# Newton chains of three norms with their operand and intermediate in PSUM, and a first product by halves

## The chip, the cores and the metric

The kernel runs on one core of a Trainium2 chip. The metric is the device time of one execution in microseconds (us); lower is better. TensorE (PE) multiplies, VectorE (DVE), ScalarE (ACT) and GpSimd (POOL) do the elementwise work, and nearly all transfers are issued from SyncE's queue (SP).

## The reference

A hybrid encoder layer is applied to two sequences of 512 and 2048 tokens (2560 rows, D = 1024) in float32, with shared weights:

```
h    = rmsnorm(x, norm_g);  proj = h @ w_in                 # queries, keys, values, gates of all branches
o_a  = gla_branch(...)      # gated linear attention forward and backward, summed, rmsnorm over 128 per head
o_b  = diff_attention(...)  # softmax(s0) - lam * softmax(s1), times v, rmsnorm over 128 per head
o_c  = memory_cross_attention(...)                          # 256 memory tokens, normed with mem_norm_g
x    = x + (sum_i sigmoid(gate_i) * ((o_i * silu(z_i)) @ w_branch_i)) @ w_out
y    = rmsnorm(x, final_norm_g)
```

Each rmsnorm needs 1 / sqrt(mean square + eps) per row, or per row and head.

## The kernel before

The kernel is written engine by engine with explicit semaphores, as six phases one after the other; within a phase every engine works through its own list in order.

`phase_project` (0 to some 715 us of the profile) norms 20 tiles of 128 token rows and 4 of memory rows, transposes them on PE into `tp` (PSUM), splits each into a rounded high part (`h_hi`, ACT) and a rest (`h_lo`, DVE), splits the weights in the same way (`w_hi` or `wv_hi` by ACT or DVE, `w_lo` or `wv_lo` by POOL at L500), and forms each product from three matmuls (`product3`, L190 to L192). For one tile, `norm(n)` on DVE takes the sum of squares that ACT left in `stat` (L344), computes the reciprocal root (L440 and `rsqrt`, L180 to L185) and scales the tile into `xn` (L444). DVE's order at the start is norm 0, low 0, norm 1, norm 2, low 1, norm 3, low 2, low 3. PE's is transpose 0, the first product, transpose 1, product 1, transpose 2, and so on. Tile n+2 of x is loaded by SP only after norm n, in one queue with the weight pieces.

`phase_gla_forward` (to some 1825 us) and `phase_gla_backward` (to some 2107 us) run the recurrence tile by tile, and fill PE with dense products for the gates (`Dense`, L744), whose weights are split by ACT (L689) and POOL (L715). In the backward phase one tile is, on PE: `o_ps` (L1253), `d_ps` (L1257), 24 x 2 dense matmuls with a transpose (L1240) between. L1253 of a tile waits for DVE's state and sum (L1297, L1302) of the tile before. On DVE, in order: the gate product of the last dense unit (L704), state, `total` (L1302), its square (L1305), the reduction (L1306), the reciprocal root (L1307, then `rsqrt`), four scalings (L1312), L704 for the next unit, the gated output (L1278, L1280) and the gate (L1270). ACT's list holds a sigmoid of the gate tile `z` (L1331) ahead of the copies that DVE waits for (L1338). SP's list stores a dense unit after DVE's L704, then, at the end of a chunk of 8 units, issues 16 loads of h (L651, L652), then the next `z`, then the next tile.

`phase_diff` (some 2116 to 2843 us) makes scores on PE (L1579, L1580) into two PSUM buffers, which DVE empties with bias and maximum (L1718); ACT exponentiates; DVE and POOL combine the two softmaxes (L1741 on DVE, L1541 and L1545 on POOL); PE transposes and multiplies by v (L1593, L1604). Once in each group of 512 queries (20 groups, 16 of them of the long sequence) `normalise(g)` computes four reciprocal roots per row from `n_ps` (L1748, L1750, `rsqrt`), POOL builds a diagonal from them (L1557), PE spreads it (L1617), and DVE scales the output (L1761, L1764).

`phase_cross` and `phase_merge` follow. The merge has a fourth norm which the change leaves alone.

`rsqrt(step, dve, out, v, tmp)` is a first guess by integer arithmetic and three Newton steps: 11 DVE instructions on 1 or 4 elements per partition, each of which waits for the one before (`Chain`). All operands are columns of `stat` in SBUF.

Of the kernel before, what the change touches and what calls it, by code (L numbers as in the profile page):

```python
# [7 lines left out]
I32 = mybir.dt.int32  # L8
ALU = mybir.AluOpType
# [3 lines left out]
P = 128  # L13
D = 1024
KT = D // P
# [5 lines left out]
CH = 512  # L21
EPS = 1e-6
LAMBDA_INIT = 0.2

H = 4
GK = 64
GV = 128
# [150 lines left out]
def rsqrt(step, dve, out, v, tmp):  # L178

    step(dve.tensor_scalar(tmp.bitcast(I32), v.bitcast(I32), 1, None, ALU.logical_shift_right))  # L180
    step(dve.tensor_scalar(out.bitcast(I32), tmp.bitcast(I32), -1.0, float(0x5F3759DF), ALU.mult, ALU.add))
    for _ in range(3):
        step(dve.tensor_tensor(tmp, out, out, ALU.mult))
        step(dve.scalar_tensor_tensor(tmp, tmp, -0.5, v, ALU.mult, ALU.mult))
        step(dve.scalar_tensor_tensor(out, tmp, 1.5, out, ALU.add, ALU.mult))  # L185


# [8 lines left out]
def phase_project(nc, used, h, early, w_zg, w2, ident, x_all, gains, ident_dram, w_stream, w_narrow, w_values, w_mem, w_mem_values, hT_hi, hT_lo, featT, featT_lo, narrowT, values,  # L196
                  memkT, mem_v):

    with ExitStack() as ctx:
        m = Mem(nc, ctx, "proj")  # L200
        HD = 64
        BANKS, TT, COLS, SLOTS, OUTS, NC = 4, CH // P, W // P, 2, 3, TOK // CH
# [27 lines left out]
        h_hi, h_lo = h  # L230
# [3 lines left out]
        wv_hi, wv_lo = (m.sb(f"wv_{s}", [P, 2, KT, W], FP32R) for s in ("hi", "lo"))  # L234
        out = m.sb("out", [P, OUTS, CH])
# [5 lines left out]
        stat = m.sb("stat", [P, 2, 4])  # L241
        acc = m.ps("acc", [P, BANKS, CH])
        tp = m.ps("tp", [P, 2, 2, 512])
# [3 lines left out]
        hi_resident = m.sem("hi_resident")  # L247
# [8 lines left out]
        lo_ready = m.sem("lo_ready")  # L256
# [176 lines left out]
        def _(dve):  # L433
            def norm(n):
                b = n % 2
                step = Chain(dve, steps, n * (RSQRT_STEPS + 1))
                dve.wait_ge(squares, n + 1)
                if n in (0, TOK // P):
                    dve.wait_ge(mem_gain_in if n else gain_in, 16)
                step(dve.tensor_scalar(stat[:, b, 1:2], stat[:, b, 0:1], 1.0 / D, EPS, ALU.mult, ALU.add))  # L440
                rsqrt(step, dve, stat[:, b, 2:3], stat[:, b, 1:2], stat[:, b, 3:4])
                if n >= 2:
                    dve.wait_ge(transposed, n - 1)
                dve.scalar_tensor_tensor(xn[:, b], x[:, b], stat[:, b, 2:3], gain[:, 1 if n >= TOK // P else 0], ALU.mult, ALU.mult).then_inc(normed, 1)  # L444
# [58 lines left out]
        def _(pe):  # L503
# [8 lines left out]
            def first_product():  # L512
                tok = slice(0, P)
                pe.wait_ge(hi_ready, 1)
                pe.wait_ge(hi_resident, COLS)
                for k in range(KT):
                    pe.matmul(acc[:, 0], h_hi[:, 0, k, tok], wv_hi[:, 0, k], start=k == 0, stop=False)
                pe.wait_ge(lo_ready, 1)
                for k in range(KT):
                    pe.matmul(acc[:, 0], h_lo[:, 0, k, tok], wv_hi[:, 0, k], start=False, stop=False)  # L520
                pe.wait_ge(lo_split, COLS)
                for k in range(KT):
                    done = pe.matmul(acc[:, 0], h_hi[:, 0, k, tok], wv_lo[:, 0, k], start=False, stop=k == KT - 1)
                done.then_inc(unit_done, 1)
# [596 lines left out]
def phase_gla_backward(nc, used, h, early, ahead, ident, v_dram, o_dram, qb_dram, kb_dram, decb_dram, gain_dram, item_hi, item_lo, hT_hi, hT_lo, w_zg, zg):  # L1121

    with ExitStack() as ctx:
        m = Mem(nc, ctx, "glab")
        S, L, PAIRS = 2, 3, H // 2
# [7 lines left out]
        v = m.sb("v", [P, L, H, GV])  # L1133
# [5 lines left out]
        stat = m.sb("stat", [P, 4, H])  # L1139
# [7 lines left out]
        t_ps = m.ps("t_ps", [P, S, H, P])  # L1147
# [12 lines left out]
        gated = m.sem("gated")  # L1160
# [105 lines left out]
        def _(dve):  # L1266
# [15 lines left out]
            for n in range(N):  # L1282
                b = n % L
# [17 lines left out]
                step = Chain(dve, steps, n * STEPS + 1)  # L1301
# [2 lines left out]
                                       o[:, b].rearrange("p (a z v) -> p z a v", z=2, v=GV), ALU.add))  # L1304
                step(dve.tensor_tensor(sq[:, :, :], total[:, :, :], total[:, :, :], ALU.mult))  # L1305
                step(dve.tensor_reduce(stat[:, 0], sq[:, :, :], AXX, ALU.add))  # L1306
                step(dve.tensor_scalar(stat[:, 1], stat[:, 0], 1.0 / GV / GK, EPS, ALU.mult, ALU.add))  # L1307
                rsqrt(step, dve, stat[:, 2], stat[:, 1], stat[:, 3])
                if n >= S:
                    dve.wait_ge(turned, n - S + 1)  # L1310
                for h in range(H):
                    done = dve.scalar_tensor_tensor(normed_o[:, n % S, h], total[:, h], stat[:, 2, h:h + 1], gain[:, :], ALU.mult, ALU.mult)  # L1312
                done.then_inc(normed, 1)
# [39 lines left out]
def phase_diff(nc, used, ahead, front, ident, v_dram, lambda_dram, gain_dram, zg, item_hi, item_lo):  # L1353

    with ExitStack() as ctx:
        m = Mem(nc, ctx, "diff")
        HD, G, LAG, TMAX, KC, SLOTS = 64, 4, 5, max(SEQS), 512, 3
# [11 lines left out]
        k, q_high, q_low, table = ahead.k, ahead.q_high, ahead.q_low, ahead.table  # L1369
        p = front.p  # L1370
        v = m.sb("v", [P, 2, TMAX // P, P])
# [18 lines left out]
        stat = m.sb("stat", [P, 4, G])  # L1390

        s_ps = m.ps("s_ps", [P, 2, 2, KC])
        t_ps = m.ps("t_ps", [P, 2, G * P])
# [303 lines left out]
        def _(dve):  # L1697
# [46 lines left out]
            def normalise(g):  # L1744
                step = Chain(dve, norm_steps, g * NORM_STEPS)
                if g:
                    dve.wait_ge(diag_ready, g)
                step(dve.scalar_tensor_tensor(stat[:, 0], sums[:, g % 4, :, 0], EPS, sums[:, g % 4, :, 0], ALU.mult, ALU.mult))  # L1748
                dve.wait_ge(squares_summed, g + 1)
                step(dve.scalar_tensor_tensor(stat[:, 1], n_ps[:, 0:G], 1.0 / P, stat[:, 0], ALU.mult, ALU.add))  # L1750
                rsqrt(step, dve, stat[:, 2], stat[:, 1], stat[:, 3])

            def scale_output(g):
                dve.wait_ge(spread, g + 1)
# [680 lines left out]
```

## Time and profile before

| | |
|---|---|
| median of 3 runs | 3529.4 us (3525.36 to 3530.46) |
| profiled execution, its own time | 3529.79 us |
| its span, first to last instruction | 3528.0 us |
| PE busy | 3374.4 us (96%) |
| DVE busy | 2072.1 us (59%) |
| ACT busy | 1329.8 us (38%) |
| POOL busy | 1216.9 us (34%) |
| mean granted clock of TensorE | 0.982 |

The profiled execution is 1.8 us longer than its span (what lies around it) and 0.4 us above the median of the runs. A busy share is an average over six phases; which engine is late in a phase is read from the waits of that phase.

### The profile page before, as it was taken

To read this page: it belongs to the slowest core of one execution; us is meant where nothing else is said; L and a number is where in the kernel's file an instruction comes from. 1 tells how busy PE (TensorE), PEld (TensorE's weight loads), DVE (VectorE), ACT (ScalarE), POOL (GpSimd) and SP (SyncE) were. 2 spreads that over 40 slices of the span, in tenths; PEclk is the share of its full clock that TensorE was granted. 3 is DMA by queue.
4 is the path that set the end of the run, shared out by engine and by line. 5 is a ranking of instruction groups with operands and counts; after the bars stand their busy time and mean duration, and the time that the engine had idled before them with its cause. 6 is when DMAs were issued, how large, how long until landed. Compare 5 with 4: busy or idle time off the path is not lost. (4 is left out here: it accounts for less than half of the span.)

```text
span 3528.0 us, 46814 instructions
## 1 busy us (share of the span) xinstructions
PE 3374.4 (96%) x16944; PEld 2629.1 (75%) x16944; DVE 2072.1 (59%) x4688; ACT 1329.8 (38%) x2165; POOL 1216.9 (34%) x511
## 2 busy tenths in 40 slices
PE   7999999999999999999999987999999978999998
PEld 5888888877888888888877774666666555888887
DVE  3322312226646655665658788988988745666554
ACT  2111111123433433343323235666666645333332
POOL 2322412343333333333333335676677623000000
PEclk9999999999999999999999998999999999999999
DMA  6544545463453543543348975121221165676662
GB/s 205 178 155 178 178 151 177 165 232 122 140 176 119 180 138 118 176 134 125 121 142 275 303 226 154 57 81 37 72 61 54 42 242 203 238 239 199 200 215 81
DMA packets 317891, 554.64 MB, mean 157 GB/s; under 512 B 35421, under 2 KB 114525, under 8 KB 317662
## 3 DMA queue, kind: packets, MB, share of 16 engines
q1 hardware_dynamic: 266510, 471.26, 40.8%
q10 hardware_dynamic: 51152, 80.38, 6.3%
q8 instruction: 136, 2.23, 0.3%
q14 instruction: 93, 0.76, 0.1%
HBM read 382.03 MB, written 169.50 MB: 156 GB/s over the span
## 5 line engine op out<-in xcount | busy, mean ns | idle before, releaser
L715 POOL TENSOR_TENSOR glaf_w_lo<-early_raw,glaf_w_hi 128x1024 fp32r<-128x1024 f32 x140 | 345.9, 2471 | 711.8 <-ACT glaf_w_hi L689 711.8
L744 PE MATMUL glaf_dense_acc<-h_hi,glaf_w_hi 128*128 128x512 f32 x1120 | 452.6, 404 | 4.1 <-ACT glaf_dense_out L698 4.1
L744 PE MATMUL glaf_dense_acc<-h_lo,glaf_w_hi 128*128 128x512 f32 x1120 | 439.3, 392 | 0.0
L744 PE MATMUL glaf_dense_acc<-h_hi,glaf_w_lo 128*128 128x512 f32 x1120 | 437.5, 392 | 0.0
L1718 DVE CUSTOM_DVE_ANT_0 front_p<-diff_s_ps,ahead_table 128x512 f32<-128x512 f32 x544 | 345.6, 686 | 49.6 <-PE diff_s_ps L1580 47.6
L500 POOL TENSOR_TENSOR proj_w_lo<-early_raw,proj_w_hi 128x1024 fp32r<-128x1024 f32 x84 | 204.4, 2436 | 479.3 <-DVE proj_w_hi L462 479.3
L1541 POOL TENSOR_SCALAR front_p<-front_p,diff_ratio 128x1024 f32<-128x1024 f32 (+1 forms) x80 | 269.0, 3362 | 174.3 <-DVE diff_ratio L1738 174.3
L1661 ACT ACTIVATE front_p<-front_p,diff_neg_max 128x2048 f32<-128x2048 f32 (+1 forms) x160 | 278.8, 1743 | 38.5 <-DVE diff_neg_max L1728 38.4
L1579 PE MATMUL diff_s_ps<-ahead_k,ahead_q_high 128*128 128x512 f32 x544 | 246.7, 453 | 34.6 <-DVE diff_mx L1718 25.4
L1604 PE MATMUL diff_oT_ps<-diff_aT,diff_v 128*128 128x512 f32 x544 | 273.8, 604 | 6.2 <-ACT diff_aT L1655 6.2
L1110 DVE COPY_PREDICATED glaf_att<-glaf_picked,glaf_att_ps 128x256 f32<-128x256 int32 x280 | 147.3, 526 | 216.5 <-PE glaf_att_ps L876 209.7
L190 PE MATMUL proj_acc<-h_hi,proj_w_hi 128*128 128x512 f32 x672 | 262.8, 391 | 0.0
L192 PE MATMUL proj_acc<-h_hi,proj_w_lo 128*128 128x512 f32 x672 | 261.6, 389 | 0.0
L191 PE MATMUL proj_acc<-h_lo,proj_w_hi 128*128 128x512 f32 x672 | 261.5, 389 | 0.0
L744 PEld LDWEIGHTS glaf_dense_acc<-h_hi,glaf_w_hi 128*128 128x128 f32 x1120 | 211.9, 189 | 53.9 <-issue 7.9
L744 PEld LDWEIGHTS glaf_dense_acc<-h_hi,glaf_w_lo 128*128 128x128 f32 x1120 | 211.1, 188 | 46.2
L744 PEld LDWEIGHTS glaf_dense_acc<-h_lo,glaf_w_hi 128*128 128x128 f32 x1120 | 212.3, 190 | 40.3
L1593 PEld LDWEIGHTS diff_t_ps<-all_ident,diff_a 128*128 128x128 f32 x1088 | 134.2, 142 | 122.9 <-issue 99.3
L1580 PE MATMUL diff_s_ps<-ahead_k,ahead_q_low 128*128 128x512 f32 x544 | 218.6, 402 | 0.0
L1655 ACT ACTIVATE diff_aT<-diff_t_ps 128x512 f32<-128x512 f32 x272 | 158.9, 592 | 150.9 <-PE diff_t_ps L1593 150.9
L382 ACT ACTIVATE proj_out<-proj_acc 128x512 f32<-128x512 f32 (+1 forms) x93 | 55.7, 598 | 413.7 <-PE proj_acc L192 395.4
L462 DVE CAST proj_w_hi<-early_raw 128x1024 fp32r<-128x1024 f32 x84 | 59.6, 715 | 250.1 <-PE proj_acc L192 250.1
(215 smaller groups left out, 7385.5 us busy)
## 6 DMA issues: line engine op xcount, KB each, us to landing
early_raw<-in_w_zg SPq DMA_DIRECT2D x180, 512.0 KB, 4.4
early_raw<-in_w_stream SPq DMA_DIRECT2D x80, 512.0 KB, 3.6
scratch_zg<-glaf_dense_out SPq DMA_DIRECT2D x140, 256.0 KB, 2.3
items_raw<-in_w_br SPq DMA_DIRECT2D x120, 256.0 KB, 2.9
merge_gate<-scratch_zg SPq DMA_DIRECT2D x120, 256.0 KB, 3.2
scratch_featT<-proj_out ACTq DMA_DIRECT2D x80, 256.0 KB, 2.2
items_br_hi<-scratch_item_hi SPq DMA_DIRECT2D x60, 256.0 KB, 5.8
items_br_lo<-scratch_item_lo SPq DMA_DIRECT2D x60, 256.0 KB, 6.6
```

What stands on the lines that cost most here:

```text
L190: pe.matmul(out, a_hi, b_hi, start=first, stop=False)
L191: pe.matmul(out, a_hi, b_lo, start=False, stop=False)
L192: return pe.matmul(out, a_lo, b_hi, start=False, stop=last)
L500: pool.tensor_tensor(lo, raw_of(n), hi, ALU.subtract).then_inc(lo_split, 1)
L715: pool.tensor_tensor(self.w_lo[:, s], self.raw[:, u % self.RAW], self.w_hi[:, s], ALU.subtract).then_inc(self.lo_split, 1)
L744: done = pe.matmul(self.acc[:, u % self.banks], a, x, start=i == 0, stop=i == self.PER - 1)
L1541: pool.tensor_scalar(p[:, o.slot, 1, half], p[:, o.slot, 1, half], ratio[:, o.slot:o.slot + 1], None, ALU.mult).then_inc(far_scaled, 1)
L1579: pe.matmul(s_ps[:, chunk % 2, i], q_high[:, b, i, cols], k[:, key % KS, i], start=True, stop=False)
L1580: done = pe.matmul(s_ps[:, chunk % 2, i], q_low[:, b, i, cols], k[:, key % KS, i], start=False, stop=True)
L1604: pe.matmul(oT_ps[:, :], v[:, o.head % 2, kt], aT[:, unit % 2], start=kt == 0, stop=kt == o.nk - 1).then_inc(values_done, 1)
L1661: act.activation(p[:, o.slot, i, 0:o.T], p[:, o.slot, i, 0:o.T], ACT.Exp, bias=neg_max[:, o.slot, i:i + 1], scale=SLOPES[o.h], accum_out=s ...
L1718: dve.tensor_tensor_reduce(out=p[:, n.slot, i, c * KC:(c + 1) * KC], in0=s_ps[:, (n.c0 + c) % 2, i], in1=table[:, start:start + KC], scale ...
```

## The change

The two norms that are computed from SBUF (projection, backward) and the one that already reads PSUM (difference attention) now write the mean square `v` to PSUM and keep the intermediate `tmp` there; only the result stays in SBUF. The Newton step is reordered; each of its two-input instructions now has one input in PSUM or both. The PSUM columns are borrowed: `tp` of the tile's own buffer in the projection, `t_ps` of the tile's own buffer in the backward phase, columns 4 to 11 of `n_ps` in difference attention. Two waits come with that: `lo_ready` in the projection, and in the backward phase `gated`, with the old wait on `turned` moved ahead of the chain. The first product of the projection starts as soon as the first 256 of its 512 weight columns are there.

```diff
+def rsqrt_by_psum(step, dve, out, v, tmp):
+    step(dve.tensor_scalar(tmp.bitcast(I32), v.bitcast(I32), 1, None, ALU.logical_shift_right))
+    step(dve.tensor_scalar(out.bitcast(I32), tmp.bitcast(I32), -1.0, float(0x5F3759DF), ALU.mult, ALU.add))
+    for _ in range(3):
+        step(dve.scalar_tensor_tensor(tmp, v, -0.5, out, ALU.mult, ALU.mult))
+        step(dve.tensor_tensor(tmp, tmp, out, ALU.mult))
+        step(dve.scalar_tensor_tensor(out, tmp, 1.5, out, ALU.add, ALU.mult))
...
-                step(dve.tensor_scalar(stat[:, b, 1:2], stat[:, b, 0:1], 1.0 / D, EPS, ALU.mult, ALU.add))
-                rsqrt(step, dve, stat[:, b, 2:3], stat[:, b, 1:2], stat[:, b, 3:4])
+                if n >= 2:
+                    dve.wait_ge(lo_ready, n - 1)
+                v, tmp = (tp[:, b, 0, i:i + 1] for i in range(2))
+                step(dve.tensor_scalar(v, stat[:, b, 0:1], 1.0 / D, EPS, ALU.mult, ALU.add))
+                rsqrt_by_psum(step, dve, stat[:, b, 2:3], v, tmp)
...
-                pe.wait_ge(hi_resident, COLS)
-                for k in range(KT):
-                    pe.matmul(acc[:, 0], h_hi[:, 0, k, tok], wv_hi[:, 0, k], start=k == 0, stop=False)
+                for half in range(2):
+                    cols = slice(half * CH // 2, (half + 1) * CH // 2)
+                    pe.wait_ge(hi_resident, (half + 1) * COLS // 2)
+                    for k in range(KT):
+                        pe.matmul(acc[:, 0, cols], h_hi[:, 0, k, tok], wv_hi[:, 0, k, cols], start=half == 0 and k == 0, stop=False)
...
-                step(dve.tensor_scalar(stat[:, 1], stat[:, 0], 1.0 / GV / GK, EPS, ALU.mult, ALU.add))
-                rsqrt(step, dve, stat[:, 2], stat[:, 1], stat[:, 3])
                 if n >= S:
+                    dve.wait_ge(gated, n - S + 1)
                     dve.wait_ge(turned, n - S + 1)
+                var, tmp = (t_ps[:, n % S, 0, i * H:(i + 1) * H] for i in range(2))
+                step(dve.tensor_scalar(var, stat[:, 0], 1.0 / GV / GK, EPS, ALU.mult, ALU.add))
+                rsqrt_by_psum(step, dve, stat[:, 2], var, tmp)
...
-                step(dve.scalar_tensor_tensor(stat[:, 1], n_ps[:, 0:G], 1.0 / P, stat[:, 0], ALU.mult, ALU.add))
-                rsqrt(step, dve, stat[:, 2], stat[:, 1], stat[:, 3])
+                var, tmp = (n_ps[:, i * G:(i + 1) * G] for i in range(1, 3))
+                step(dve.scalar_tensor_tensor(var, n_ps[:, 0:G], 1.0 / P, stat[:, 0], ALU.mult, ALU.add))
+                rsqrt_by_psum(step, dve, stat[:, 2], var, tmp)
```

## Rows read from the trace of the kernel before

In rows 1 the columns are: stretch, its length, busy us (and instructions) of PE, PEld, DVE, ACT and POOL, granted clock, DMA share, GB/s. In rows 2: who waited for whom, us in total, times, longest. In rows 3: line, engine, operation, count, duration in ns as min/median/max, first and last start, form. In rows 4 to 6: start, duration in us, engine, line, form, count, and in brackets the idle time before and what ended it.

**Rows 1.** Busy time by stage: projection, backward phase, long groups of difference attention.
```profile
60.00:710.00 650.00, 650.00 (x2948) 534.16 (x2947) 164.71 (x405) 114.26 (x196) 188.54 (x78) 1.00 0.49 172
1825.00:2107.00 282.00, 265.47 (x1358) 211.59 (x1359) 226.54 (x518) 85.40 (x118) 99.52 (x41) 0.95 0.82 270
2222.00:2798.00 576.00, 561.84 (x2484) 374.78 (x2483) 517.70 (x1447) 388.26 (x514) 401.91 (x147) 1.00 0.18 54
```
**Rows 2.** PE's waits, in the stretches 0:60, 1815:2130 and 2130:2880.
```profile
PE proj_tp L509 <- DVE proj_xn L444: 12.6, 2, 9.9
...
PE glab_o_ps L1253 <- DVE glab_total L1302: 5.2, 2, 4.7
PE glab_dense_acc L744 <- POOL glab_w_lo L715: 4.1, 2, 2.5
...
PE diff_s_ps L1579 <- DVE diff_mx L1718: 22.5, 35, 2.9
```

**Rows 3.** DVE's durations by line, over the whole span.
```profile
L181 DVE TENSOR_SCALAR diff_stat<-diff_stat x20: 170/2320/2328, 2148.6 to 2835.3; 128x4 int32<-128x4 int32 x20
L1307 DVE TENSOR_SCALAR glab_stat<-glab_stat x20: 170/838/2299, 1840.6 to 2102.6; 128x4 f32<-128x4 f32 x20
L1750 DVE SCALAR_TENSOR_TENSOR diff_stat<-diff_n_ps,diff_stat x20: 160/161/163, 2148.2 to 2834.9; 128x4 f32<-128x4 f32 x20
L704 DVE TENSOR_TENSOR glab_dense_out<-glab_dense_acc,glab_dense_out x40: 676/684/692, 1846.2 to 2109.2; 128x512 f32<-128x512 f32 x40
L1718 DVE CUSTOM_DVE_ANT_0 front_p<-diff_s_ps,ahead_table x544: 676/685/693, 2118.6 to 2798.1; 128x512 f32<-128x512 f32 x182
L1764 DVE TENSOR_TENSOR diff_y<-diff_y,diff_z x20: 691/2650/2657, 2154.7 to 2841.4; 128x512 f32<-128x512 f32 x20
```

**Rows 4.** Timeline of the start.
```profile
15.10 9.45 POOL L500 TENSOR_TENSOR proj_wv_lo<-early_raw,proj_wv_hi 128x1024 fp32r<-128x1024 f32 x4 [0.21 <-ACT proj_wv_hi L398]
15.15 2.32 DVE L185 SCALAR_TENSOR_TENSOR proj_stat<-proj_stat 128x1 f32<-128x1 f32 x1
16.81 3.41 PE L517 MATMUL proj_acc<-proj_wv_hi,h_hi 128*128 128x512 f32 x8 [4.96 <-ACT proj_wv_hi L398]
21.88 1.98 PE L523 MATMUL proj_acc<-proj_wv_lo,h_hi 128*128 128x512 f32 x8
25.18 1.28 DVE L444 SCALAR_TENSOR_TENSOR proj_xn<-proj_x,proj_stat,proj_gain 128x1024 f32<-128x1024 f32 x1
26.52 1.97 PE L509 MATMUL proj_tp<-all_ident,proj_xn 128*128 128x128 f32 x8 [2.67 <-DVE proj_xn L444]
31.28 0.77 PE L190 MATMUL proj_acc<-proj_wv_hi,h_hi 128*128 128x512 f32 x1 [2.79 <-issue]
```

**Rows 5.** Timeline of the backward phase: second tile, third chunk load, last two tiles.
```profile
1845.21 0.72 PE L1253 MATMUL glab_o_ps<-glab_state,glab_qb 64*128 64x128 f32 x8
...
2007.59 0.71 PE L1253 MATMUL glab_o_ps<-glab_state,glab_qb 64*128 64x128 f32 x8
2022.21 0.69 DVE L1280 TENSOR_TENSOR glab_out_lo<-glab_prod,glab_out_hi 128x512 fp32r<-128x512 f32 x1 [6.75 <-ACT glab_out_hi L1338]
2025.37 1.23 PE L1253 MATMUL glab_o_ps<-glab_state,glab_qb 64*128 64x128 f32 x8 [4.65 <-DVE glab_total L1302]
...
2081.27 0.71 PE L1253 MATMUL glab_o_ps<-glab_state,glab_qb 64*128 64x128 f32 x8
2094.09 0.71 PE L1253 MATMUL glab_o_ps<-glab_state,glab_qb 64*128 64x128 f32 x8
```

**Rows 6.** Timeline of one long group of difference attention.
```profile
2261.54 2.39 POOL L1545 TENSOR_TENSOR diff_a<-front_p 128x1024 f32<-128x1024 f32 x1
2261.63 2.32 DVE L181 TENSOR_SCALAR diff_stat<-diff_stat 128x4 int32<-128x4 int32 x1
...
2277.53 0.50 PE L1579 MATMUL diff_s_ps<-ahead_k,ahead_q_high 128*128 128x512 f32 x1 [0.22 <-DVE diff_mx L1718]
2282.14 0.50 PE L1579 MATMUL diff_s_ps<-ahead_k,ahead_q_high 128*128 128x512 f32 x1 [0.75 <-DVE diff_mx L1718]
```

## The prediction

> **What bounds the kernel now.** I read the busy time by stage first. In the projection PE is busy 650.00 of 650 us: there the kernel is PE's, and DVE with its 164.71 us can't matter. In the backward phase PE has 265.47 of 282 us and DVE 226.54; in the long groups of difference attention PE has 561.84 of 576 and DVE 517.70 [rows 1]. So little is to be had in any phase, and only where PE stands idle. Then PE's waits: three places name DVE. At the start PE waits for the normed tile, in the backward phase twice for DVE's sum and twice for a weight split, in difference attention 35 times for the score buffers that DVE empties [rows 2].
>
> Next, the durations of the instructions that the change touches. A step of the chain works on 1 or 4 elements and takes 0.16 to 0.17 us, but L181 has a median of 2.32 us in difference attention, and L1307 reaches 2.30 in the backward phase [rows 3]. The timeline shows what they have in common: at 15.15 us a chain step lasts 2.32 us while POOL works through four splits of 9.45 / 4 = 2.36 us each, and at 2261.63 a step lasts 2.32 us inside POOL's 2.39 us instruction [rows 4, 6]. A DVE step whose operands are all in SBUF is held until POOL's instruction ends. DVE instructions with one of two inputs in PSUM are not: L704 never exceeds 0.69 us in 40, L1718 never 0.69 in 544, though POOL is busy 99.52 of 282 and 401.91 of 576 us there, while L1764 with both inputs in SBUF has a median of 2.65 us [rows 1, 3]. This is the price that the change can take away: PSUM operands pull the whole chain out of POOL's way.
>
> **The change, part by part.** The number of instructions in a chain stays (a mean square and 11 steps). Their cost in PSUM: L1750 reads PSUM and takes 161 ns, the same as its neighbours in SBUF (0.16 us) [rows 3]. Nothing in the trace shows DVE writing PSUM. From below I take -0.01 us a step, since L704, with an input in PSUM, is no slower than a form in SBUF (L1764's shortest, 691 against 684 ns). From above I take a whole second step, 0.16 us, or 12 x 0.16 = 1.9 us a chain. I take 0, by L1750, the row nearest in form.
>
> A rule of the Trainium skill speaks against this. VectorE: DVE Perf Modes, section "The TRN2 errata", gives an instruction from PSUM 120 fixed cycles and one from SBUF 58; at its 0.96 GHz that is 0.065 us more a step, an estimate of 0.8 us a chain. L1750's 161 ns disagree. By the rule the sum below would lose about a third of its second and third terms, and the time would be near 3505.
>
> *Start.* The second tile's chain begins at 14.21 us in the profile, and four of its steps are held; its scaling L444 starts only at 25.18, transposes at 26.52, product 1 at 31.28 [rows 4]. Without holds the chain takes 2.3 us and ends at 16.5. L444 has two SBUF inputs and is now the one held, to 15.10 + 2.36 = 17.46, and ends at 18.74. POOL's next split, the last that the first product needs, moves behind it: 18.74 to 21.10 instead of 17.46 to 19.82. The first product starts at 13.0 instead of 16.81, when the first tile's high part is there; its second half waits for the fourth weight piece, as before (16.8), so its eight further matmuls lie in time that was idle. Its last part starts at 21.10 instead of 21.88 and ends 1.98 later [rows 4], at 23.1. So the halves in themselves bring at most 0.8 us, and POOL's split limits them. The transposes follow at once, 23.1 to 24.1 (at full clock; at 26.52 they took 1.97 us for 8, which is the 1.2 GHz level, after an idle of 2.67). From their end to product 1 the profile has 31.28 - 28.49 = 2.79 us, for ACT's copy and DVE's subtraction. Product 1 starts at 26.9, 4.4 us earlier. Norm 2 is through DVE by 24.7 (its scaling held once more), ahead of that subtraction. SP's queue gains too, as the third x tile waits for norm 1. What follows is the old pattern, and from 60 us PE is never idle, so the 4.4 us stay. If norm 2's scaling met a second split, 2.4 of them would go; if PE kept its clock in product 1, some 2.4 would come on top. Term: 4.4 (2 to 7).
>
> *Later norms of the projection.* PE is never idle beside them: 0. The new wait on `lo_ready` is on DVE's own earlier work: 0.
>
> *Backward phase.* PE's tile period undisturbed is 2094.09 - 2081.27 = 12.82 us. From the second tile's start to the last one's, 248.88 us, 18 periods are 230.8: 18.1 us are lost [rows 5]. How: at each load of an h chunk the gate tile's load is queued behind 16 others, ACT's list stands, and DVE idles (6.75 us until L1280 at 2022.21). PE was ready for its next L1253 at 2025.37 - 4.65 = 2020.7 and had to wait for DVE's sum, which follows L1280; the whole tile takes 17.78 us [rows 5]. DVE had no slack to bridge this, for between loads it has only some 0.7 us a tile to catch up. I summed the chain's holds tile by tile from the timeline: 36 us over 20 tiles (the row of L1307 alone has a median of 0.84 against 0.17 [rows 3]). Without them DVE would catch up by up to 1.8 us more a tile. Part returns, as L1305 and L1312 have two SBUF inputs and can be held instead, so I count 1.4. In the four tiles between two loads that is 5.6 us, more than the 4.65 for which PE stood; POOL's late splits (4.1 us in all [rows 2]) hang on loads queued behind the same list and come earlier with it. I take 13 of 18.1, as each load still costs DVE its 6 to 7 us and one of the three may find it late. Bounds: 5 (only the third load) to 18. The wait on `gated` is DVE's own, and `turned`, moved ahead, was already waited for by DVE's item before it: 0. Behind them on DVE would stand L704 and the state that L1253 needs.
>
> *Difference attention.* In each long group the chain is held once, 2.32 - 0.17 = 2.15 us, by L1545 [rows 3, 6]. PE then waits 0.22 and 0.75 us one and two turns later; that pair stands in 14 of 16 long groups. Counted between starts at PE's undisturbed spacing the loss is 1.3 us a group. After the change DVE leaves the chain at 2263.5 instead of 2265.7, waits about 0.4 for scores, and reaches L1764 some 1.8 earlier; L1545 still holds that one, but it ends 1.8 earlier. As 1.8 exceeds 1.3, both waits go; PE's own work is late next, 561.84 of 576 us being busy already. 14 x 1.1 (between 0.97 and 1.3) = 15.4, with bounds 8 and 20. Short groups and the last ones, whose chains are hardly held: 0.6. POOL's diagonal comes 1.9 us earlier, with slack before and after.
>
> **Sum.** 4.4 + 13 + 15.4 + 0.6 = 33.4 us from the profiled 3529.79, that is 3496.4; the median of the runs is 0.4 lower, so 3496.
>
> **What no row shows.** The chain also has single-input steps (L180, L181) with an operand in PSUM, and none of that form lies beside POOL here. SBUF — State Buffer, section "Who interferes with whom", has VectorE hold the pair that it shares with GpSimd only with two SBUF inputs or in a two-port mode. By that they would run free, as my sum has it.
>
> **Rivals.** (1) *The hold moves on.* L1312 in the backward phase, L1764 in difference attention, L444 at the start wait for POOL in the chain's stead, and DVE comes out no earlier. For it: L1764's median of 2.65, and 401.91 us of POOL. Against it: POOL's instruction is finite, and a chain of 2.3 us outlasts nearly all of it. Price: the backward phase keeps all but 4, difference attention gives 8, the start 3: 15 us, 3514. (2) *The holds are hidden anyway:* PE's waits stay, since they come from PE's own buffers or from DMA. For it: PE's 96%; z's load is DMA's. Then only the start: 3525. (3) *The single-input steps are still held,* so that the change doesn't do all it says: L181 is the one held in difference attention. The start keeps 4.4 and the backward phase half: 3518. (4) *Slower: each step in PSUM costs a second step.* At 12 x 0.16 = 1.9 us a chain the 2.15 us of a long group are just paid back; beyond some 0.18 us a step DVE is later than before in every group. At 0.25 a step, 3.0 us a chain, DVE loses 0.85 in 16 groups and 1.2 in 20 tiles, all of it PE's wait: 14 + 24 - 4 = 34 us slower, 3563. Against it: L1750's 161 ns. (5) *More than forecast:* all 18 in the backward phase, 20 in difference attention, 7 at the start: 3485.
>
> **How the numbers follow.** Forecast 0.6, rival 1 0.15, rival 2 0.05, rival 3 0.08, rival 4 0.04, rival 5 0.08. The forecast's own range is 3488 to 3507. The range for 8 in 10 goes from 3485 to 3518, which takes in the skill's price and rivals 1, 3 and 5. 0.2% is 7 us, about what a measurement of this kernel can tell from none: the forecast and rivals 1, 3 and 5 are faster by more (0.91, of which 0.01 goes to rival 1 falling short: 0.9), rival 2 is within it (0.06 with that), rival 4 slower (0.04).
>
> **What would show it.** Each chain 2.3 us long with no step over 0.2; L444 of tile 1 held and ending near 18.7, product 1 near 27; 12.8 us for nearly every backward tile, also at the chunk loads, with DVE less than 15 us late; no wait of L1579 for L1718 one or two turns after a closing, and a group of 38.0 to 38.3 us instead of 39.3. It is wrong if chain steps in PSUM take over 0.2 us, if L1312 or L1764 grows by what the chain lost, or if PE's waits persist with DVE early.

## The result: 3481.5 us, faster than forecast

| | before | after |
|---|---|---|
| median of the runs | 3528.4 us (3525.4 to 3530.5, 4 runs) | 3481.5 us (3480.1 to 3484.9, 4 runs) |
| profiled execution: time, span | 3529.8, 3528.0 | 3480.1, 3478.3 |
| mean granted clock | 0.982 | 0.987 |

The ratio is 0.9872, with a 95% interval of 0.9859 to 0.9886. The prediction was 3496 with a range of 3485 to 3518: direction and mechanism held, the size didn't, and the time lies 3.5 us below the range. In the profiled execution 49.7 us went where 33.4 were forecast.

The first view is again the busy time by stretch, for the changed kernel. The first three rows answer to [rows 1]; the last is a stretch that holds long groups of difference attention alone.

```profile
60.00:710.00 650.00, 650.00 (x2948) 534.23 (x2947) 164.20 (x406) 114.30 (x196) 189.81 (x79) 1.00 0.49 173
1825.00:2107.00 282.00, 267.95 (x1379) 212.61 (x1377) 220.06 (x550) 90.25 (x133) 100.35 (x45) 0.97 0.85 276
2222.00:2798.00 576.00, 563.74 (x2527) 376.16 (x2525) 480.38 (x1428) 385.73 (x521) 404.83 (x150) 0.99 0.21 66
...
2240.00:2640.00 400.00, 400.00 (x1801) 270.18 (x1800) 353.82 (x1047) 276.64 (x372) 289.42 (x107) 1.00 0.21 62
```

The same 400 us of the kernel before:

```profile
2240.00:2640.00 400.00, 389.93 (x1731) 260.40 (x1730) 358.65 (x1005) 270.76 (x358) 281.32 (x102) 1.00 0.20 59
```

Read the counts as well as the microseconds. PE's idle time falls by 10.1 us, but it does 1801 matmuls instead of 1731 in the same time, 4.0% more: 16 us of work. The idle time understates the loss by more than a third, and this is the trap into which the prediction fell.

PE's waits after the change, in the stretches 0:60, 1815:2130 and 2130:2880 [rows 2]. The wait of the backward phase's product for DVE's sum (5.2 us before) has no row any more, and in the last stretch L1597's wait for DVE (the old L1579's) fell from 22.5 us in 35 to 6.5 in 6.

```profile
PE proj_tp L523 <- DVE proj_xn L458: 9.9, 1, 9.9
...
PE glab_dense_acc L760 <- POOL glab_w_lo L731: 3.7, 2, 2.1
...
PE diff_s_ps L1597 <- DVE diff_mx L1736: 6.5, 6, 2.9
```

DVE's durations by line (ns, min/median/max), answering to [rows 3]: L192 is the old L181, L1783 the old L1764.

```profile
L191 DVE TENSOR_SCALAR diff_n_ps<-diff_n_ps x20: 169/170/171, 2128.3 to 2788.2; 128x4 int32<-128x4 int32 x20
L192 DVE TENSOR_SCALAR diff_stat<-diff_n_ps x20: 160/161/163, 2128.5 to 2788.4; 128x4 int32<-128x4 int32 x20
L1783 DVE TENSOR_TENSOR diff_y<-diff_y,diff_z x20: 691/2656/2665, 2134.6 to 2794.5; 128x512 f32<-128x512 f32 x20
```

And the timeline of a chain beside POOL, answering to [rows 6]:

```profile
2233.77 3.93 POOL L1559 TENSOR_SCALAR front_p<-front_p,diff_ratio 128x1024 f32<-128x1024 f32 x1 [1.18 <-DVE diff_ratio L1756]
2237.35 0.16 DVE L1766 SCALAR_TENSOR_TENSOR diff_stat<-diff_sums 128x4 f32<-128x4 f32 x1
2237.75 0.17 DVE L191 TENSOR_SCALAR diff_n_ps<-diff_n_ps 128x4 int32<-128x4 int32 x1
2237.85 2.39 POOL L1563 TENSOR_TENSOR diff_a<-front_p 128x1024 f32<-128x1024 f32 x1
2237.95 0.16 DVE L192 TENSOR_SCALAR diff_stat<-diff_n_ps 128x4 int32<-128x4 int32 x1
2238.15 0.17 DVE L194 SCALAR_TENSOR_TENSOR diff_n_ps<-diff_n_ps,diff_stat 128x4 f32<-128x4 f32 x1
```

From L192 on, the rest of the chain (to 2239.93) runs inside POOL's 2.39 us instruction, and no step of it is held. Before, L181 was held in 15 groups; L192 started inside L1563 in 15 groups too and took 0.16 us each time.

Last, where the time went, by the start of PE's first matmul of each phase (from the timelines of both kernels):

| | before | after | gained in the phase before it | forecast |
|---|---|---|---|---|
| backward phase | 1830.08 | 1824.07 | 6.0 (start and projection) | 4.4 |
| difference attention | 2116.35 | 2096.84 | 13.5 (backward) | 13 |
| cross attention | 2849.02 | 2802.11 | 27.4 (difference attention) | 16 |
| merge | 2965.12 | 2916.81 | 1.4 (cross) | 0 |
| end of the span | 3528.0 | 3478.3 | 1.4 (merge) | 0 |

### The profile page after: what moved, and what is told of

Same layout as the page of the kernel before. It is cut to its first block and busy times, and to the rows that moved or that the text cites. A ratio compares the mean times of both kernels' runs of the same rounds, so it can differ in the third digit from the quotient of the medians.

```text
span 3478.3 us, 46851 instructions
## 1 busy us (share of the span) xinstructions
PE 3356.4 (96%) x16952; PEld 2621.7 (75%) x16952; DVE 2013.1 (58%) x4688; ACT 1325.7 (38%) x2165; POOL 1219.7 (35%) x511
## 3 DMA queue, kind: packets, MB, share of 16 engines
q8 instruction: 136, 2.23, 0.3%
## 5 line engine op out<-in xcount | busy, mean ns | idle before, releaser
L514 POOL TENSOR_TENSOR proj_w_lo<-early_raw,proj_w_hi 128x1024 fp32r<-128x1024 f32 x84 | 204.6, 2437 | 479.2 <-DVE proj_w_hi L476 479.2
L1559 POOL TENSOR_SCALAR front_p<-front_p,diff_ratio 128x1024 f32<-128x1024 f32 (+1 forms) x80 | 270.3, 3379 | 174.3 <-DVE diff_ratio L1756 174.3
L1679 ACT ACTIVATE front_p<-front_p,diff_neg_max 128x2048 f32<-128x2048 f32 (+1 forms) x160 | 278.9, 1744 | 10.1 <-DVE diff_neg_max L1746 10.0
L1597 PE MATMUL diff_s_ps<-ahead_k,ahead_q_high 128*128 128x512 f32 x544 | 245.0, 450 | 18.4 <-DVE diff_mx L1736 10.8
```

Source lines behind the costliest of these rows:

```text
L514: pool.tensor_tensor(lo, raw_of(n), hi, ALU.subtract).then_inc(lo_split, 1)
L1559: pool.tensor_scalar(p[:, o.slot, 1, half], p[:, o.slot, 1, half], ratio[:, o.slot:o.slot + 1], None, ALU.mult).then_inc(far_scaled, 1)
L1597: pe.matmul(s_ps[:, chunk % 2, i], q_high[:, b, i, cols], k[:, key % KS, i], start=True, stop=False)
L1679: act.activation(p[:, o.slot, i, 0:o.T], p[:, o.slot, i, 0:o.T], ACT.Exp, bias=neg_max[:, o.slot, i:i + 1], scale=SLOPES[o.h], accum_out=s ...
```

## The experiments

### Each part alone

`only_diff`, `only_back` and `only_proj` are the kernel before with the chain in PSUM in one of the three norms; `only_halves` has the first product's halves and nothing else.

```diff
 # only_diff (normalise); only_back and only_proj in the same manner
+var, tmp = (n_ps[:, i * G:(i + 1) * G] for i in range(1, 3))
-step(dve.scalar_tensor_tensor(stat[:, 1], n_ps[:, 0:G], 1.0 / P, stat[:, 0], ...))
-rsqrt(step, dve, stat[:, 2], stat[:, 1], stat[:, 3])
+step(dve.scalar_tensor_tensor(var, n_ps[:, 0:G], 1.0 / P, stat[:, 0], ...))
+rsqrt_by_psum(step, dve, stat[:, 2], var, tmp)
```

> The kernel before with the PSUM chain in difference attention alone. Theory A (the hold of the chain alone sets PE's waits there, and a group without it takes PE's own 37.7 us, as one long group before did): 13 long groups x 1.6, the first long group 3.7 and the closing ones 2.1, together 27 us faster than before, group period 37.7. Rival B (the term was sized right, and what came above it was carried in by the earlier phases): 16 us faster, group period 38.2.

> The kernel before with the PSUM chain in the backward phase alone. Theory A: 13 to 14 us faster, all of it between the phase's first matmul and the next phase's; the wait of 4.65 us at the third chunk load is gone. Rival B (DMA at the chunk loads sets the stalls, and the gain needed the earlier start): under 7 us faster, the wait stays. Rival C (the gain of this phase moved the later ones too): over 20.

> The kernel before with the PSUM chain in the projection alone, the first product whole. Theory A: tile 1's scaling starts near 16.6 instead of 25.2, the first product ends as before near 23.8, product 1 starts near 27.5: 4 to 5 us faster. Rival B (the halves carried the start): 1 to 2 us faster.

> The kernel before with the first product by halves alone, all chains in SBUF. Theory A: the transposes of tile 1 still wait for its scaling, which is held until 26.5, so 0 (within 1 us). Rival B: the first product ends 2 us earlier and the time follows, 2 us faster. Rival C: the eight further matmuls with their weight loads cost, 1 us slower.

| kernel | median, us | ratio to before (95%) | phase of its own, from the timeline |
|---|---|---|---|
| only_diff | 3503.9 | 0.9931 (0.9919 to 0.9944) | 732.7 to 709.9 |
| only_back | 3517.1 | 0.9971 (0.9958 to 0.9983) | 286.3 to 274.5 |
| only_proj | 3520.9 | 0.9981 (0.9972 to 0.9990) | 1830.1 to 1826.3 |
| only_halves | 3526.9 | 1.0002 (0.9993 to 1.0011) | 1830.1 to 1830.2 |

The last column is the phase's length before and with the part, or for the two parts of the projection the start of the backward phase. The three chains add up to 0.0117 of the time, 41 us, and the halves alone to nothing that shows; together they gave 0.0128, 45. The intervals of the parts are wide enough to hold the difference, so no interaction is shown. The largest is difference attention, 24 us where the sum had 16: the group period of 37.7 us is that of theory A, but the 3.7 us that it wanted from the first long group did not come. `only_back` gave 11.8 us in its phase, somewhat less than the 13 to 14 expected, with 0.6 us left of PE's wait for DVE's sum; `only_proj` brought product 1 to 27.65 us as expected and gave 3.8 us up to the backward phase (4 to 5 expected). In `only_diff` the same 400 us look as they do with the whole change:

```profile
2240.00:2640.00 400.00, 399.64 (x1806) 270.65 (x1805) 352.14 (x1049) 277.92 (x372) 294.31 (x107) 1.00 0.22 65
```

### Is it PSUM, or the order of the steps?

`chain_in_sbuf` keeps all of the change (new order of the Newton products, earlier waits, halves) and takes only the operand and the intermediate back to SBUF.

```diff
-v, tmp = (tp[:, b, 0, i:i + 1] for i in range(2))
+v, tmp = stat[:, b, 1:2], stat[:, b, 3:4]
-var, tmp = (t_ps[:, n % S, 0, i * H:(i + 1) * H] for i in range(2))
+var, tmp = stat[:, 1], stat[:, 3]
-var, tmp = (n_ps[:, i * G:(i + 1) * G] for i in range(1, 3))
+var, tmp = stat[:, 1], stat[:, 3]
```

> The changed kernel with its new order of the Newton steps, its earlier waits and the halves of the first product, but with the chain's operand and intermediate back in SBUF in all three norms. Theory: PSUM is what counts, the order and the waits bring nothing: steps are held again (2.3 us once a long group, period 39.3; about 36 us in the backward phase; the start's four), 3527 within 3. Rival: the order (the first product no longer squares its own result) or the earlier waits carry the gain: 3482 to 3500.

3524.8 us, ratio 0.9997 (0.9988 to 1.0006): the gain is gone. PSUM is the whole of it, and the new order, the waits and the halves give nothing that shows without it.

`seed_in_sbuf` is the changed kernel with one value less in PSUM: the intermediate between the two seed steps.

```diff
-step(dve.tensor_scalar(tmp.bitcast(I32), v.bitcast(I32), 1, None, ALU.logical_shift_right))
-step(dve.tensor_scalar(out.bitcast(I32), tmp.bitcast(I32), -1.0, float(0x5F3759DF), ...))
+step(dve.tensor_scalar(seed.bitcast(I32), v.bitcast(I32), 1, None, ALU.logical_shift_right))
+step(dve.tensor_scalar(out.bitcast(I32), seed.bitcast(I32), -1.0, float(0x5F3759DF), ...))
```

> The changed kernel, but the intermediate between the two seed steps (shift, then multiply and add) lies in SBUF in all three norms: the second seed step is then the one step of a chain with all operands in SBUF, and it has a single input of 1 to 16 elements. Theory: a single small input in SBUF is enough to be held until POOL's instruction ends, and the hold of a long group comes back whole: that step 2.3 us, period 39.3, 23 us lost in difference attention; in the backward phase one step in twelve can meet POOL, so a third to a half of its 13.5 comes back lost, 5 us; the start loses 1 to 2. 3510 (3503 to 3516). Rival: only steps with two inputs in SBUF are held; the step stays at 0.17 us and the time at 3481.

3514.4 us, ratio 0.9965 (0.9953 to 0.9978). That is 33 us above the changed kernel, 70% of the whole gain, for one step with a single input (4 elements in the two phases that lost time). Its durations, and its place in one group:

```profile
L192 DVE TENSOR_SCALAR glab_stat<-glab_stat x20: 169/170/2220, 1836.6 to 2093.4; 128x4 int32<-128x4 int32 x20
L192 DVE TENSOR_SCALAR diff_stat<-diff_stat x20: 169/2322/2332, 2140.2 to 2825.2; 128x4 int32<-128x4 int32 x20
```
```profile
2251.17 2.39 POOL L1563 TENSOR_TENSOR diff_a<-front_p 128x1024 f32<-128x1024 f32 x1
2251.26 2.33 DVE L192 TENSOR_SCALAR diff_stat<-diff_stat 128x4 int32<-128x4 int32 x1
```

The same step with its input in PSUM took 0.16 us at the same place (2237.95 above). The rival, that only two inputs in SBUF are held, is out for 4 elements. The Trainium skill, SBUF — State Buffer, section "Who interferes with whom", names this case too: a `tensor_scalar` with its operands in SBUF can enter a two-port mode and then contends with GpSimd. The trace agrees: 2.33 us against 0.16.

With 1 element it is otherwise: in the projection this step (128x1, SBUF to SBUF) started 12 times inside POOL's L514 and took 0.15 us each time, and before, L181 of that size did so 11 times: at 123.83 us it takes 0.15 with 0.60 us of POOL's instruction left, and the two-input L183 behind it, at 124.02, is held for the rest (0.43 us). So the expectation's 1 to 2 us at the start had no hold behind it, and the prediction's sentence that a step with all operands in SBUF is held is too wide.

In the backward phase the cost, 9 us (272.8 to 281.8), is above the 5 expected, although only one of the chain's twelve steps can be held there. L192's total says why: 20 of them took 15.9 us, where free ones take 3.2, so one step caught 12.7 us of holds, a third of what the whole chain had caught before (36).

### How much is a microsecond of DVE worth?

`delay5` and `delay11` are the changed kernel with the mean-square step of difference attention repeated, so that DVE's list is longer by a known time with no hold. `back_delay11` does it in the backward phase.

```diff
-step(dve.scalar_tensor_tensor(var, n_ps[:, 0:G], 1.0 / P, stat[:, 0], ...))
+for _ in range(12):    # delay5: range(6); NORM_STEPS is raised by 11 (5)
+    step(dve.scalar_tensor_tensor(var, n_ps[:, 0:G], 1.0 / P, stat[:, 0], ...))
```

> The same with five repeated steps, 1.0 us a group. Theory: before, a hold of 2.15 us cost 1.6 us a group, so 0.55 us of it was slack; 1.0 us then costs 0.4 to 0.5 a group, period 38.1 to 38.2, 13 x 0.45 = 6 us, 3487 to 3488. Rival A (gain from elsewhere): 3482. Rival B (no slack): 16 us, 3497. Rival C (the prediction's sizes: 1.1 us for 2.15, a slack of 1.05): nothing is lost, 3482, and then eleven steps cost no more than 15.

> The changed kernel, with the mean-square step of the chain in difference attention written eleven times more (each reads PSUM, writes PSUM, and repeats the same value). A PSUM step took 0.20 us from start to start in the changed kernel's chain (2.57 us for 13), so the chain is 2.2 us longer without any hold, which is what the hold by POOL cost before (2.15). Theory: what the change gave in difference attention is DVE's time alone; then the group's period goes back from 37.7 to about 39.3 us, 13 x 1.6 + 2 = 23 us are lost, 3504. Rival A: the gain came from elsewhere (POOL or DVE undisturbed at the shared port, the diagonal earlier); plain DVE time hurts little, period 37.7 to 38.0, 3482 to 3486. Rival B: with PE now without idle, DVE's slack is gone too and each added 2.2 us is lost whole: 16 x 2.2 = 35, 3516.

> The changed kernel with the mean-square step of the backward phase's chain written eleven times more (SBUF to PSUM, the same value), which is some 2.2 us of DVE a tile without any hold; the holds were 1.8 a tile (36 over 20 tiles) before. Theory: DVE's time alone made the loss: at each chunk load it falls behind by 6 to 7 us and can't catch up; the phase goes back from 272.7 to 286 us or, as 2.2 is more than 1.8, up to 294: 3495 to 3503. Rival A: the gain came from transfers and splits that started earlier, and DVE's time has slack: 3481 to 3486. Rival B: DVE becomes the bound of every tile (12.1 + 0.4 us of work would be 12.5, just under PE's 12.8; if it is over, each tile loses): more than 3505.

| kernel | median, us | ratio to before (95%) | long group, us | backward phase, us |
|---|---|---|---|---|
| before | 3526.7 to 3528.4 | 1 | 39.3 | 286.3 |
| after | 3481.5 | 0.9872 (0.9859 to 0.9886) | 37.7 | 272.8 |
| delay5 | 3497.8 | 0.9917 (0.9904 to 0.9931) | 38.2 | 273.6 |
| delay11 | 3521.8 | 0.9990 (0.9981 to 0.9999) | 39.4 | 275.4 |
| back_delay11 | 3498.4 | 0.9920 (0.9908 to 0.9933) | 37.7 | 289.3 |

The long group is the time from one spread of the scale factors to the next. It is read from the timeline of PE, here before, after, `delay5` and `delay11` in turn:

```profile
2269.59 1.02 PE L1617 MATMUL diff_n_ps<-diff_diag,diff_ones 128*128 128x512 f32 x2
2308.87 1.02 PE L1617 MATMUL diff_n_ps<-diff_diag,diff_ones 128*128 128x512 f32 x2
```
```profile
2283.84 1.02 PE L1635 MATMUL diff_n_ps<-diff_diag,diff_ones 128*128 128x512 f32 x2
2321.55 1.02 PE L1635 MATMUL diff_n_ps<-diff_diag,diff_ones 128*128 128x512 f32 x2
```
```profile
2288.30 1.02 PE L1635 MATMUL diff_n_ps<-diff_diag,diff_ones 128*128 128x512 f32 x2
2326.53 1.02 PE L1635 MATMUL diff_n_ps<-diff_diag,diff_ones 128*128 128x512 f32 x2
```
```profile
2298.28 1.02 PE L1635 MATMUL diff_n_ps<-diff_diag,diff_ones 128*128 128x512 f32 x2
2337.70 1.02 PE L1635 MATMUL diff_n_ps<-diff_diag,diff_ones 128*128 128x512 f32 x2
2377.14 1.02 PE L1635 MATMUL diff_n_ps<-diff_diag,diff_ones 128*128 128x512 f32 x2
```

In the long groups the theory holds at both doses. 1.0 us more of DVE costs 0.5, 2.2 us cost 1.7, and the period of `delay11` is that of the kernel before: the group had a slack of about 0.5 us, and all beyond it is paid. The wait shows the trap of the prediction once more. With `delay11` PE's waits for DVE in 2240:2640 are these, exactly as in the kernel before, 0.96 us in each group that is 1.7 us longer:

```profile
PE diff_s_ps L1597 <- DVE diff_mx L1736: 9.6, 20, 0.8
```

The totals, however, missed: `delay11` lost 40 us where the theory had 23, `delay5` 16 where it had 6. The intervals between spreads, `delay11` against the changed kernel, show where: the 13 long groups lost 22.8 us, as expected, but the first two intervals 7.1, the third 2.0, the last two 4.6 and the stretch ahead of the first spread 1.9. (In `delay5`: 6.7 in the long ones, 5.5 elsewhere.) So the short groups show no slack for DVE: the first two intervals lost 3.7 and 3.4 us for 2.2 added, the last two 2.3 each. Why the first two lost more than was added was not tried. The real holds of the kernel before seldom fell there, and its first two intervals are as long as the changed kernel's. The expectation had counted the 13 long groups and 2 us more.

`back_delay11` landed inside its 3495 to 3503: with 2.2 us more a tile and no hold in the chain, the backward phase takes 289.3 us, 3 more than before, where the holds were 1.8 a tile. PE's product starts in the changed kernel, around the second and third chunk load [rows 5]:

```profile
1953.76 0.71 PE L1269 MATMUL glab_o_ps<-glab_state,glab_qb 64*128 64x128 f32 x8
1970.29 0.72 PE L1269 MATMUL glab_o_ps<-glab_state,glab_qb 64*128 64x128 f32 x8
...
2008.75 0.72 PE L1269 MATMUL glab_o_ps<-glab_state,glab_qb 64*128 64x128 f32 x8
2024.89 0.72 PE L1269 MATMUL glab_o_ps<-glab_state,glab_qb 64*128 64x128 f32 x8
```

and in `back_delay11`, where the first load costs time again as well (12.8 undisturbed):

```profile
1864.21 0.72 PE L1269 MATMUL glab_o_ps<-glab_state,glab_qb 64*128 64x128 f32 x8
1879.78 1.22 PE L1269 MATMUL glab_o_ps<-glab_state,glab_qb 64*128 64x128 f32 x8 [2.68 <-issue]
1895.52 0.71 PE L1269 MATMUL glab_o_ps<-glab_state,glab_qb 64*128 64x128 f32 x8
...
2002.31 0.72 PE L1269 MATMUL glab_o_ps<-glab_state,glab_qb 64*128 64x128 f32 x8
2019.71 1.23 PE L1269 MATMUL glab_o_ps<-glab_state,glab_qb 64*128 64x128 f32 x8 [3.38 <-DVE glab_total L1318]
```

### Is there more to be had, and what are the halves worth?

`scale_in_psum` takes the one instruction that is still held in every long group, L1783, out of POOL's way too.

```diff
-dve.scalar_tensor_tensor(y[:, :], outT[:, :], gain[:, 0:1], n_ps[:, :], ...).then_inc(y_ready, 1)
+dve.scalar_tensor_tensor(n_ps[:, :], outT[:, :], gain[:, 0:1], n_ps[:, :], ...).then_inc(y_ready, 1)
-dve.tensor_tensor(y[:, :], y[:, :], z[:, g % 2], ALU.mult).then_inc(gated, 1)
+dve.tensor_tensor(y[:, :], n_ps[:, :], z[:, g % 2], ALU.mult).then_inc(gated, 1)
 # sum_squares on PE waits for gated instead of y_ready
```

> The changed kernel; in difference attention the scaled output goes from the first of the two scaling instructions to the second through PSUM (in place over the spread factors) instead of SBUF, so the product with z has one input in SBUF and should no longer be held by POOL: 0.75 us instead of 2.65 in 16 groups. The next group's sums of squares wait for that product instead of the first scaling. Theory: PE has no wait left in the long groups, period 37.7, so 1.9 us less of DVE a group brings nothing there; in the third and fourth group, where PE still waits for the score buffers, 1 to 2 us: 3480 (3477 to 3482). Rival A: DVE still sets the period in part, every group gains: 3465 or less. Rival B: PE's sums of squares, now waiting for the product with z, are late: 3485 or more.

> The changed kernel with the first product of the projection whole again; the three chains stay in PSUM. Theory: with the chain in place the halves are worth something, though alone they brought nothing, since only then is the second tile's norm early enough that PE's part counts: up to the backward phase the changed kernel had 6.0 us, the projection's chain alone 3.8, so 2 us are lost, 3483 to 3484. Rival A: what the prediction had, at most 0.8: 3482. Rival B: the halves, which run at half clock early, cost as much as they bring: 3481 or less.

`scale_in_psum`: 3481.5 us, ratio 0.9870 (0.9857 to 0.9884), the same as the changed kernel. The hold is gone (first row), DVE works 19 us less in 400, and PE's row does not move:

```profile
L1783 DVE TENSOR_TENSOR diff_y<-diff_n_ps,diff_z x20: 691/691/692, 2132.2 to 2793.2; 128x512 f32<-128x512 f32 x20
```
```profile
2240.00:2640.00 400.00, 400.00 (x1802) 270.30 (x1801) 334.40 (x1046) 276.85 (x371) 289.80 (x106) 1.00 0.21 62
```

PE is the bound of the long groups now; another 1.9 us of DVE a group buys nothing. None of these kernels is faster than the changed one by more than the scatter.

`no_halves`: 3485.6 us in 4 runs that lie between 3480.1 and 3490.2, ratio 0.9887 (0.9871 to 0.9902), which overlaps the changed kernel's interval, so it can't choose between its theory and its rivals. Its profiled span is 3478.3, the same as the changed kernel's, and up to the backward phase it took 1822.0 against 1824.1. Together with `only_halves`, the halves aren't shown to be worth anything. The start of both kernels shows what they change. With the halves:

```profile
13.04 2.07 PE L533 MATMUL proj_acc<-proj_wv_hi,h_hi 128*128 128x256 f32 x8 [1.17 <-ACT h_hi L364]
16.48 2.07 PE L533 MATMUL proj_acc<-proj_wv_hi,h_hi 128*128 128x256 f32 x8 [1.37 <-ACT proj_wv_hi L409]
18.36 3.62 PE L536 MATMUL proj_acc<-proj_wv_hi,h_lo 128*128 128x512 f32 x8
21.77 2.17 PE L539 MATMUL proj_acc<-proj_wv_lo,h_hi 128*128 128x512 f32 x8
27.52 0.47 PE L201 MATMUL proj_acc<-proj_wv_hi,h_hi 128*128 128x512 f32 x1 [2.70 <-issue]
```

Without them:

```profile
17.07 3.75 PE L531 MATMUL proj_acc<-proj_wv_hi,h_hi 128*128 128x512 f32 x8 [5.17 <-ACT proj_wv_hi L409]
20.62 2.23 PE L534 MATMUL proj_acc<-proj_wv_hi,h_lo 128*128 128x512 f32 x8
22.68 2.00 PE L537 MATMUL proj_acc<-proj_wv_lo,h_hi 128*128 128x512 f32 x8
28.25 0.76 PE L201 MATMUL proj_acc<-proj_wv_hi,h_hi 128*128 128x512 f32 x1 [2.70 <-issue]
```

The halves bring product 1 forward by 0.73 us, close to the 0.8 at most of the prediction. But with them the next eight matmuls (L536) run at the 1.2 GHz level, 3.62 us for 8, and not in 2.23. In the eight traces with halves these matmuls took 2.9 to 3.6 us, in the five without 2.0 to 3.0. Whether this clock is what eats the 0.73 us is not shown: `only_proj`, without halves, began the product behind product 1 at 36.93 us, and `no_halves`, with the same code up to there, at 38.94. The mean granted clock in 10:60 is 0.90 with them and 0.93 without; before it was 0.83.

## Why the prediction was off, step by step

**What held.** The price in PSUM: steps of 4 elements that write to PSUM take 170 ns, those that read it and write SBUF 161, and a chain of difference attention 2.38 us against 2.34 in the four groups where it was free before. That is within 0.1 us of the 0 taken, and far from rival 4. The Trainium skill's fixed cost of 120 cycles against 58 (VectorE: DVE Perf Modes, section "The TRN2 errata") would have made it 0.8 us a chain and 3505 us; the measurement decides against it for this form. That a hold ends with POOL's instruction is shown by `seed_in_sbuf` (2253.59 and 2253.56 us), and that single-input steps are freed too by the chain inside L1563 (rival 3 out). Rival 1 was right in one part: L1783 and L458 are still held (2.66 us, and 1.90 at 16.59), but DVE reaches them earlier and the time is not given back. Rival 2 is out.

**Backward phase: 13 forecast, 13.5 measured.** The reasoning held, as `back_delay11` shows from the other side. Its picture was too rosy in one place: two of the three loads still cost 3.7 and 3.3 us (tiles of 16.5 and 16.1 us), while nearly every other tile took 12.8.

**Start: 4.4 forecast, 6.0 measured.** L458 ended at 18.5 (forecast 18.74) and product 1 began at 27.52 (forecast 26.9). The prediction had named the surplus, "if PE kept its clock in product 1": the product behind it is 4.7 us earlier (38.41 against 43.11), product 1 itself 3.8, at a clock of 0.90 instead of 0.83. The rest can't be told from scatter: `only_proj` and `no_halves` are the same code up to the backward phase and reached it at 1826.3 and 1822.0.

**Difference attention: 16 forecast, 27.4 measured.** This is the step that failed: "Counted between starts at PE's undisturbed spacing the loss is 1.3 us a group", and from it "14 x 1.1 (between 0.97 and 1.3) = 15.4". The term is mis-sized, not misunderstood. A group fell from 39.3 to 37.7 us, 1.6, and in 13 groups the sum is 21.3; the last long group gave 2.0 more. `only_diff` shows the same 21.1 and 2.0, so this is the chain's alone. The 0.97 were PE's recorded idle times, and the 1.3 a spacing around those two stands only.

The count between starts gives more when it is done again. The matmuls of L1579 start 0.36 us after the transposes of L1593 where nothing stands, as at 2278.92, but 0.82 and 1.35 us after them at the two stands (2277.53 and 2282.14 [rows 6]):

```profile
2276.71 0.60 PE L1593 MATMUL diff_t_ps<-all_ident,diff_a 128*128 128x128 f32 x4
...
2278.56 0.60 PE L1593 MATMUL diff_t_ps<-all_ident,diff_a 128*128 128x128 f32 x4
2278.92 0.48 PE L1579 MATMUL diff_s_ps<-ahead_k,ahead_q_high 128*128 128x512 f32 x1
...
2280.79 0.60 PE L1593 MATMUL diff_t_ps<-all_ident,diff_a 128*128 128x128 f32 x4
```

That is 0.46 and 0.99 us of loss where 0.22 and 0.75 are recorded as idle, since the record of the transposes (0.60 us) reaches 0.24 us past the start that was due. A third place, at 2271.74, comes 0.44 us after its transposes and has no idle at all: 0.08 more. Together 1.53 us, which is the period's 1.5 to 1.6. A shorter check is the period itself: the trace of before has one long group in which PE has no wait (2231.8 to 2269.6, 37.8 us) among groups of 39.3. The chain just ahead of it, at 2222.35, was held as in the others (2.29 us), so that group shows PE's own pace and that a hold can fall where it costs nothing; why it did there was not tried. Either reading would have given 14 x 1.5 = 21, and a sum of 39 us: near 3490. The prediction also bounded the gain too low ("8 and 20").

What was missed in all is 49.7 - 33.4 = 16.3 us: 11.4 here (7.7 in the later long groups and the closing ones, and 3.7 in the first long group, below), 1.6 at the start, 0.5 in the backward phase and 2.8 behind difference attention.

**Unforecast: 3.7 us in the first long group.** It took 41.5 us before and 37.8 after, but 41.6 in `only_diff`, 42.0 in `only_back`, 40.3 in `only_halves`, 41.9 in `chain_in_sbuf`, 39.3 in `only_proj`, 37.8 in `seed_in_sbuf`, 39.0 in `scale_in_psum`: this is no work of one part. The clock goes with it. In the 32 us from the start of that group's idle turns on (2196:2228 before, 2176:2208 after) the rows are

```profile
2196.00:2228.00 32.00, 23.67 (x86) 15.29 (x87) 29.55 (x82) 17.12 (x21) 20.73 (x9) 0.89 0.28 82
```
```profile
2176.00:2208.00 32.00, 25.93 (x104) 16.47 (x105) 30.34 (x93) 18.97 (x23) 23.84 (x10) 0.95 0.28 83
```

Two things differ, this clock and PE's wait for the score buffers in the group, 7.2 us before and 4.9 after. `only_proj` tells them apart: it has the wait of the changed kernel, 4.9, and the clock of the kernel before, 0.89, and takes 39.3 us. So the clock is worth some 1.5 us here, and with the 2.3 of the wait the 3.7 are there. `chain_in_sbuf`, with a wait of 4.9 too, has a clock of 0.79 in the same stretch of the group and takes 41.9. `only_diff`, with the old 41.6, has 0.89 and 7.2 as before. This is an estimate from single traces; what decides which way the group falls was not tried. So 3.7 of the 27.4 us can't be put down to the chain.

**Cross attention and merge: 0 forecast, 1.4 each.** Neither phase is changed. In the other kernels they vary as much (114.7 to 116.1 us from cross to merge in `only_back` and before, 561.4 to 563.1 from merge to the end), so no cause is put to it.

## What to carry to other kernels

Measure a loss inside a loop by its period, against an iteration of the same trace that is free of it, or by the spacing of starts: the sum of PE's recorded idle times came to 0.96 us where the loop lost 1.6. One small DVE instruction with all operands in SBUF is enough to give most of the gain back when GpSimd runs beside it (33 of 47 us here), so look in the trace at every step of a chain for a hold, and not only at those with two inputs. And price a microsecond by place: here an added one cost nothing up to a slack of 0.5 us in long groups and at least itself in short ones, and a removed one gave nothing once PE was busy 400 of 400 us.

## What was not expected of the hardware

- Not every instruction of POOL holds DVE. L1766 has both inputs in SBUF (one tensor, read twice) and started 15 times inside POOL's L1559, a `TENSOR_SCALAR` of 3.9 us, as at 2237.35 above: 0.16 us each time. The same L1766 started three times inside a `TENSOR_TENSOR` of POOL (L1563 or L1567) and was held to its end each time: 0.48, 0.54 and 1.23 us. L1563, 2.39 us on the same 128x1024 elements as L1559, also held L1783 in all 16 long groups and, in `seed_in_sbuf`, L192 in 15. So it counts which instruction of POOL lies there, not how long POOL is busy.
- Nor is every small DVE instruction in SBUF held. L1745, a `TENSOR_REDUCE` from SBUF to SBUF, started nine times inside L1563 with 0.27 us or more of it left and took 0.15 to 0.16 us, while L1746 behind it, single-input with 2 elements, was held at 2138.03 (0.47 us); the single-input steps of 1 element were free too, as said at `seed_in_sbuf`.
- Writing to PSUM costs DVE a small instruction's 8 to 9 ns (170 against 161, 128x4). Reading from it costs nothing that shows in a two-input step (161 against 161 to 162 in SBUF), and the single-input L192 is even shorter from PSUM, 161 ns against 170 when free in SBUF.
- More work at the start can go with a lower clock: with the halves PE's 8 matmuls behind them took 2.9 to 3.6 us in eight traces, without them 2.0 to 3.0 in five.
